# Two layers of attention on one core: whom each engine waits for between stages, and work of the next stage placed in the stage before

## The reference

```python
x = x + concat(rwkv7(xn), dsa(xn)) @ w_out ; x = rmsnorm(x)          # first layer
h = rmsnorm_2(x); proj = h @ w_in_2      # c_q 384, c_kv 256, k_rope 32, q_mem 256, gate 1024
q = (rmsnorm_2(c_q) @ w_uq) ; kv = rmsnorm_2(c_kv) @ w_ukv            # 12 heads, 64+32 | 64+64
s = (q_nope k_nope + rope(q_rope) rope(k_rope)) / sqrt(96) ; p = softmax(s) ; attn = p @ v
mem_out = softmax(q_mem k_mem / 8) @ v_mem       # k_mem, v_mem = rmsnorm_2(mem) @ w_mem_kv
x = x + (concat(attn, mem_out) * silu(gate)) @ w_out_2 ; out = rmsnorm_2(x)
```

## The kernel before

| stage | what it does | PE's part of it in the profiled run |
|---|---|---|
| a | projection of layer 1 | 0 to 838 us |
| 2 | scan and sparse attention of layer 1 | 838 to 2041 |
| mix1 | output projection of layer 1, two norms, transposes of the normed rows | 2041 to 2253 |
| 4 | input projection of layer 2: 32 weight blocks, norms of the two latents | 2253 to 2632 |
| heads | queries, keys and values of 12 heads, keys and values of the memory | 2632 to 2853 |
| 5 | attention (24 units of 8 steps), then memory attention (32 units) | 2853 to 4012 |
| mix2 | output projection of layer 2 and the last norm | 4012 to 4203 |

## Time and profile before

### The profile page before, as it was taken

The page is one execution under the profiler, slowest core; times in us unless marked ns, Lnnn a source line. Parts: engine busy times, 40 slices in busy tenths (PEclk is TensorE's granted clock), DMA queues, the critical chain, the costliest instruction groups (busy, mean ns, idle before and its releaser), DMA issues. The chain is left out here.

```text
span 4203.6 us, 76236 instructions
## 1 busy us (share of the span) xinstructions
PE 3898.8 (93%) x31096; PEld 2744.4 (65%) x31096; DVE 2701.7 (64%) x5092; ACT 2074.8 (49%) x3077; POOL 1280.9 (30%) x1016
## 2 busy tenths in 40 slices
PE   6999999999888999889798999797999999999889
PEld 5777765756666666666586878684555555555577
DVE  5656677767777787888654332445777777777443
ACT  3434597768677777866333221222333333333431
POOL 2212222322544454453110000002445444454200
PEclk9999999999999999999899999898999999999999
DMA  3334232322211212122465333663223232231343
GB/s 122 113 103 146 68 104 92 117 65 58 67 36 38 51 43 53 46 57 70 143 215 200 120 138 133 242 207 95 66 56 89 56 79 56 63 82 29 104 143 110
DMA packets 389534, 407.18 MB, mean 97 GB/s; under 512 B 115937, under 2 KB 288417, under 8 KB 388929
## 3 DMA queue, kind: packets, MB, share of 16 engines
q1 hardware_dynamic: 388096, 399.00, 32.7%
q10 hardware_dynamic: 1088, 3.32, 0.2%
HBM read 249.74 MB, written 152.47 MB: 96 GB/s over the span
## 5 line engine op out<-in xcount | busy, mean ns | idle before, releaser
L144 ACT ACTIVATE PT<-psum 128x1024 f32<-128x1024 f32 x384 | 394.3, 1027 | 667.1 <-PE psum L134 666.6
L172 DVE TENSOR_REDUCE m<-psum 128x1 f32<-128x1024 f32 x384 | 468.1, 1222 | 281.8 <-PE psum L134 281.7
L134 PE MATMUL psum<-xc,wah 128*128 128x512 f32 x1600 | 530.9, 413 | 11.2 <-DVE xc L148 5.8
L148 POOL TENSOR_TENSOR part<-PT 128x1024 f32<-128x1024 f32 x144 | 341.8, 2374 | 473.5 <-DVE all L148 379.3
L148 POOL TENSOR_TENSOR Lm<-gm,cst 64x512 f32<-64x512 f32 x192 | 258.2, 1345 | 380.3 <-PE psum L134 194.0
L134 PE MATMUL psum<-PT,V 128*64 128x512 f32 x1536 | 371.5, 605 | 0.0
L134 PEld LDWEIGHTS psum<-xc,wah 128*128 128x128 f32 x1600 | 301.7, 192 | 97.1 <-issue 22.9
L134 PE MATMUL psum<-hc,w4h 128*128 128x512 f32 x1024 | 320.1, 394 | 8.7 <-DVE w4l L148 8.7
L134 PE MATMUL psum<-xc,wal 128*128 128x512 f32 x800 | 318.0, 397 | 0.0
L145 ACT ACTIVATE bias<-score,cand,cols 128x2048 bf16<-128x2048 f32 (+4 forms) x155 | 244.5, 1578 | 78.8 <-DVE cand L155 75.0
L145 ACT ACTIVATE sgn<-score,cand,cols 128x1920 bf16<-128x1920 f32 (+4 forms) x155 | 227.9, 1470 | 58.7 <-DVE cand L155 57.4
(11 more groups left out here) (379 smaller groups left out, 8847.8 us busy)
## 6 DMA issues: line engine op xcount, KB each, us to landing
raw_a<-in_w_a SPq DMA_DIRECT2D x50, 512.0 KB, 3.7
raw_w<-in_w_in SPq DMA_DIRECT2D x32, 512.0 KB
QNh<-scr_qnh SPq DMA_DIRECT2D x48, 256.0 KB, 4.9
QRh<-scr_qrh SPq DMA_DIRECT2D x96, 128.0 KB, 4.7
QNl<-scr_qnl SPq DMA_DIRECT2D x48, 256.0 KB, 6.3
xin<-in_x SPq DMA_DIRECT2D x16, 512.0 KB
scr_AR<-AR SPq DMA_DIRECT2D x32, 256.0 KB, 2.2
scr_BK<-BK SPq DMA_DIRECT2D x32, 256.0 KB, 2.2
```

Of the source, the lines that this page charges most:

```text
L134: return self.e.matmul(out, a, b, start=start, stop=stop, skip_group_check=True)
L144: return self.e.activation(out, src, f, bias=bias, scale=scale)
L148: return self.e.tensor_tensor(out, a, b, op) if self.e else self.vector(out)
L172: return self.e.tensor_reduce(out, a, AX, op, negate=negate) if self.e else self.vector(a)
```

## The change

- `phase_end`: only SP still waits for `ended["sp"]`. PE waits for nobody at the changes 2, 3 and 5 (mix1 to 4, 4 to heads, 5 to mix2), and for ACT, DVE and POOL at the others. Waits on the pieces themselves stand in their place, where a tile or a bank would be written too early.
- mix1 has a new piece, `first4`, which splits block 0 of stage 4's weights. Stage 4 begins without it, and the small constant it took from POOL is made in stage a.
- stage 4 has three new pieces, `wq` 0 to 2: the three blocks of `wqh`, `wql`. The heads begin with blocks 3 (loaded) and 4.
- the heads have the first 16 `max` pieces, both rows' stores and loads, and part of the constant rows. `load_heads(0)` comes two results earlier, and the 16 use two pairs of banks in turn, not three. Stage 5 begins without them.
- the memory attention has the eight `w` pieces of mix2 (`mw`, after the units 5, 8, ... 26) and its first `split` (`my`); mix2 begins without them.
- tiles are laid out in another order, so that what is made early lies in free memory.

```diff
         def phase_end(q, me, n):
             q.drain().then_inc(*ended[me].up(n))
+            if me == "pe" and n in (2, 3, 5):
+                return
             for name in ended:
-                if name != me:
+                if name != me and (me == "sp" or name != "sp"):
                     q.wait_ge(ended[name], n)
...
+                    if top and n == 13:
+                        order += [("first4",)]
...
+        for i, s in enumerate((27, 28, 30)):
+            order_4.insert(order_4.index(("p", s, 3)) + 1, ("wq", i))
...
+                    if n < 4:
+                        q.wait_ge(mix1.dve, "o", NT - 1, 1)
+                    elif n == 4:
+                        q.wait_ge(mix1.dve, "hl", NT - 2, 1)
...
-        order_h = [("w", 0), ("c2", 0)] + [("w", i) for i in range(1, 5)] + [("c2", 1), ("mload",)]
+        order_h = [("c2", 0), ("w", 3), ("w", 4), ("c2", 1), ("mload",)]
...
+        firsts = [("first", v, b, x) for v in range(2) for b in range(4) for x in range(2)]
+        after = order_h.index(("qr", 3, 1))
+        more = [("ones",)] + [y for k in firsts for y in ([k, ("row", k[1])] if k[2:] == (3, 1) else [k])]
+        order_h = order_h[:after] + more + order_h[after:]
...
-                    if n == first_in + 5:
-
+                    if n == first_in + 3:
+                        for m in range(first_in - 2, first_in + 1):
+                            q.wait_ge(d_eh[m % 5], m)
+                            q.wait_ge(d_el[m % 5], m)
                         q.wait_ge(h_pe, "x", "v", 2, 3, 1)
                         q.wait_ge(h_dve, "w", 4)
                         load_heads(q, 0)
+                elif k[0] == "row":
+                    row_out(q, k[1])
+                    row_in(q, k[1])
...
-        order_5 = [("gat", 0), ("load", 1)] + with_row(passes[:16])
+        order_5 = [("gat", 0), ("load", 1)]
...
+        for c in range(8):
+            order_m.insert(order_m.index(("m1", 5 + 3 * c)) + 1, ("mw", c))
+        order_m.insert(order_m.index(("m3", NM - 1)), ("my", 0))
...
-            return (4, 0, 2)[n % 3] if n < 16 else 4
+            return (4, 6)[n % 2] if n < 16 else 4
```

More of the change, by code:

```diff
@@ L2019, in __init__ @@
                     if n < NT:
-                        order += [("y", n), ("split", n), ("x", n)]
-                    if n < 4:
+                        order += [("y", n)] + ([("split", n)] if top or n else []) + [("x", n)]
+                    if top and n < 4:
                         order += [("w", 2 * n), ("w", 2 * n + 1)]
@@ L2074, in mix_sp @@
                     q.dma(dst[M.rows_of(i), :], M.g[i % 3][:, :]).then_inc(*M.d_o[i % 3].up(i))
+                elif k[0] == "first4":
+                    for e in range(2):
+                        q.wait_ge(M.d_cs[e], 3)
+                    q.dma(raw_w[1][:, :, :], A["w_in2"][1]).then_inc(*d_w4[1].up(1))
                 elif k[0] == "keep" and k[1] > 3:
@@ L2512, in pool_4 @@
         def pool_4(q):
-            q.fill(eps4[:, :], 1e-6).then_inc(*b_pool.up("eps"))
+            return
         so_far = len(taken)
@@ L2534, in program @@
         SH = Stack()
-        wqh = SH.sb("wqh", [128, 12, 3, 128], FR)
-        wql = SH.sb("wql", [128, 12, 3, 128], FR)
+        cch.append(SH.sb("cch1", [128, 5, 512], FR))
+        ccl.append(SH.sb("ccl1", [128, 5, 512], FR))
         wkh = SH.sb("wkh", [128, 6, 2, 128], FR)
@@ L2551, in program @@
         sel = SH.sb("sel", [64, 128])
+        m8 = SH.two("m8", [128, 8])
+        negm = SH.two("negm", [128, 4], FR)
         d_sel = landing("sel")
@@ L2703, in pe_heads @@
                     i.then_inc(*h_pe.up("x", *k))
+                elif what == "first":
+                    max_nope(q, *k[1:])
+                    max_rope(q, *k[1:])
                 elif what == "kr":
@@ L2763, in act_heads @@
                     q.act(KS[p0:p0 + 32, cs_], bank[4][p0:p0 + 32, :], ACT.Copy).then_inc(*h_act.up("kr", c))
+                elif what == "ones":
+                    q.wait_ge(h_dve, "w", 4)
+                    for a in range(2):
+                        t = zero_row(q, 0, a)
+                    t.then_inc(*q_act.up("zero0"))
                 elif what == "mn":
@@ L2824, in dve_heads @@
                     q.tt(KS[ps, cs_], bank[4][ps, :], KE.bitcast(F32)[ps, cs_], ALU.subtract).then_inc(*h_dve.up("krl", c))
+                elif what == "first":
+                    max_dve(q, *k[1:])
+                elif what == "ones":
+                    q.wait_ge(h_dve, "krl", 3)
+                    for a in range(2):
+                        ps = slice(64 * a + 32, 64 * a + 64)
+                        t = q.ts(KE[ps, :].rearrange("p (n t) -> p n t", n=8), rep(one[ps, :], 8), ident[ps, 64 * a + 32:64 * a + 33], None, ALU.mult)
+                    t.then_inc(*q_dve.up("ones"))
                 elif what == "mn":
@@ L2858, in program @@
         PT = S5.two("PT", [128, 4, 512], n=4)
-        m8 = S5.two("m8", [128, 8])
-        negm = S5.two("negm", [128, 4], FR)
         part5 = S5.two("part", [128, 2, 512])
@@ L3151, in act_5, with prepare @@
         def act_5(q):
-            for i in range(3):
+            def prepare(k):
+                if k[0] == "my":
+                    y_upper(q, mix2, k[1])
+                else:
+                    q.wait_ge(q_pool, "add", NST - 1)
+                    q.wait_ge(q_pool, "half", NUN - 1, 1)
+                    weight_upper(q, mix2, k[1])
+            for i in (1, 2):
                 for a in range(2):
-                    ps = slice(64 * a + 32, 64 * a + 64)
-                    t = q.act(QRl[i][ps, :].rearrange("p (n t) -> p n t", n=8), rep(one[ps, :], 8), ACT.Copy, scale=0.0)
+                    t = zero_row(q, i, a)
             t.then_inc(*q_act.up("zero"))
             for k in order_5:
+                if k[0] in ("mw", "my"):
+                    prepare(k)
+                    continue
                 if k[0] == "s":
```

203 lines of the change are left out of this document (127 added, 76 removed).

## The result

The changed kernel takes 4185.5 us, the median of 13 runs (4182.11 to 4193.85); the kernel before, in 13 runs beside them, 4196.01 (4191.09 to 4201.80, and one of 4478.17, for which nothing here shows a cause). The ratio is 0.9978, 95% interval 0.9971 to 0.9985: 10.5 us faster. That lies in the predicted range (4159 to 4192), 7.5 us above the predicted 4178. The direction is the forecast one, the size a little over half of the 19.3 us.

What follows compares the result with a forecast made beforehand. PE, busy 93% of the span, was taken to bound the kernel, with gaps at stage changes. Terms 0 − 2.3 − 3 − 12.5 − 7.5 + 6 = −19.3 us, from median 4196.97, gave 4178; range 4159 to 4192.

Steps and rivals of the forecast that it cites:

- Change 0: First stage change: others no longer wait for SP's stores, but PE next stops for `bk`'s load; 0 (bounds 0, −2).
- Change 1: Into mix1: without the wait for SP's store, ACT, DVE and PE start earlier; −2.3 us, at worst nothing.
- Change 2: Mix1 to stage 4: 8.71 us gap goes, but block 4's landing leaves a slow-clock gap before the first sum; −3 us.
- Change 3: Stage 4 to heads: PE goes straight on, then stops for the memory's rows with seven pieces done; −12.5 us.
- Change 4: Heads to stage 5: 16 maxima made in the heads bring PE's first maximum of unit 1 earlier; −7.5 us.
- The return of the row is the price: Within change 4: row 1's trip out and back keeps SP busy until 2866.4, before it issues unit 1's loads.
- Change 5: Stage 5 to mix2: gap and slow clock save 8.4 us, eight weight pieces lengthen the memory attention by 14.3; +6.
- The carry-over: Whole kernel: the difference worked out on the profiled execution, −19.3 us, applied in full to the median, 4196.97.
- Rival A: Memory attention: each weight piece delays the y loop by a landing, 6.5 us not 1.8; 4215 us; chance 0.05.
- B: Memory attention: the weight pieces are hidden, change 5 is −8, the sum −33; 4164 us; chance 0.15.
- C: Heads to stage 5: first maxima bring nothing, since SP, held by row 1, issues loads late; 4185 us; chance 0.10.
- D: Heads' start and stage 5: gaps return as others, change 3 brings 3.3, change 4 nothing; 4194.5 us; chance 0.10.

Runs made afterwards that it cites:

- the other profile: The kernel before, unchanged, profiled a second time: 4190.37 us.
- The first profile: The kernel before, unchanged, in the profiled execution that the prediction was worked out on: 4205.36 us.
- the other (0.3 us): Changed kernel with the halves of each memory-attention weight piece apart, ACT's copy behind the unit before, DVE's subtraction a unit later: 4169.02 us, ratio 0.9934.

## Why the prediction was right or wrong

- *Change 0, worth nothing*: PE's next stop was a load behind SP's waits there too (4.95 us for `qx`). The stretch (+0.3) differs by less than its own spread, 2031.7 to 2042.9.
- *Change 1, −2.3*: −2.5, and 2.4 of idle time came back when the wait did. Right. No run shows the 0.15 that I left in for a drain: ACT's first issue came 2.48 us after DVE's end before, and 0.11 after the change (2036.67 against 2036.56).
- *Change 2, −3*: −2.3 in this profile. The gap before the sum and its slow clock were right in kind, and putting block 4 first removed both and 5.3 us. The size is less sure than it looks: in eight other profiles with the same stage 4 the stretch takes 376.3 to 378.8 us, against 378.4 and 378.7 before, so the change brought between nothing and 2.3 us; the gap before the sum is up to 4.1 us in them, where 4.3 was forecast.
- *Change 3, −12.5*: from the last `hc` product to the last rotation the stretch fell from 200.9 and 199.2 us to 188.9, so by some 11; no run puts this part back alone. PE resumed 26.3 us after the last `hc` product with seven pieces done, forecast 27.0 and seven. The stop of 3.59 for `krr` was not seen, and the 10.26 us that I counted as removed are 7.56 in the other profile.
- *Change 4, −7.5*: the step that failed. From the last rotation to POOL's first sum the stretch is 5.8 us shorter, and the chain itself came out as worked (the second `negm` 23.9 us after the last rotation, forecast 24.0; PE's maximum of unit 1 within 2 us of its forecast place), but the comparison was wrong: I set the arrival of unit 1 against its old one and gave the difference to the maxima. The kernel without them arrives as early (within 1 us, counted from the last rotation). What the stretch gained beside change 3 was the earlier place of `load_heads(0)`, 4.7 us, a term that I left out. "The return of the row is the price" fell too: it is worth some 2 us, and the rest is, as far as the traces tell, the bare load of unit 1.
- *Change 5, +6*: +9.5. The mechanism held. The price per piece was mis-sized, 2.2 net against my 1.8: PE's stops for `qmt` fell from 4.5 to 1.6 us, near the 3.3 that I took off, so it is the gross price that was low, 2.6 against 2.2. The sum had no term for the clock in the memory attention, where PE's busy time grew by 6.1 us, 0.8 per piece. The gap before mix2, 1.3, came out as forecast, and mix2 itself was 1.8 us shorter.
- *The carry-over*: I took all 19.3 us over to the median. The first profile was 8.4 above it, and the counted stop was 2.7 longer in it than in the second.
- *The time within the range*: this is partly luck. The maxima brought nothing where 7.5 us were forecast, and the place of the loads, which I had not priced, gave 4.7 of it back.

Rival A is out: a piece never cost a landing. B is out for this placement, but nearly true for the other (0.3 us). C was right about the maxima, and only partly about the reason; that its 4185 is the measured time is luck too, since it lacks the 4.7 us of the loads and has 6 for change 5 where 9.5 was measured. D, no gain at the heads' start, is out.

## What to carry to other kernels

Before placing work of the next stage in this one, ask which engine waits inside the piece: two halves on two engines belong a unit apart, or one engine's wait stands in the chain of everything behind it. Where work hides a load, moving the work does not move the load. And where one engine issues loads and stores in order, the place of a load decides which stores stand behind it: two results earlier was worth 4.7 us at the end of the heads, and all loads ahead of the first store left ACT without a buffer for 10.4 us at their start, once the memory's rows came early. Look at what the buffers behind a load do.

## What the runs showed that I had not expected

The same instructions of stages a and 2, some 2036 us, took between 2031.7 and 2042.9 us from one execution to another, and single executions of one kernel differ by 10 to 20 us (4185.0 to 4202.3 for the kernel before in one set of 22 runs): for changes of 5 us profiles must be compared by stretches, and whole times by many runs. And the stores of a row, four pieces of 512 B, were answered 6.4 to 8.3 us after the last was issued, when nothing else held SP; that is longer than the 4.7 us that a load of 128 KB took to land in the earlier trace rows.
